# Two-layer hybrid encoder on one core: RWKV blocks moved ahead of the two attention mixers, and an expert loop body of four experts in place of two

## The chip, the cores and the metric

The kernel runs on one core of a Trainium2 chip, in one launch. The metric is the device time of one execution in microseconds (us); the median of several runs is compared. The engines are named as the profile names them: PE is TensorE (matmuls), PEld its weight loads, DVE is VectorE, ACT is ScalarE, POOL is GpSimd and SP is SyncE, which here only issues DMA. "Granted clock" is the share of TensorE's full clock of 2.4 GHz that it was allowed: 1.00 is 2.4 GHz, 0.50 is 1.2 GHz.

## The reference

256 prompt tokens and 32 tokens of a later stream (288 columns in all) pass through two layers of width 1024. Each layer has four token mixers side by side, a gated sum of them, and a feed-forward part.

```python
def prompt_layer(x, p, l):                      # sample_layer: the same with carried states
    h = rmsnorm(x, p['norm_mix'][l])
    za, zb, zc, zd, zg = split_at(h @ p['w_in'][l], TOP_SIZES)
    ya, ... = rwkv_mixer(za, ...)               # A: recurrence over the tokens, then per-head norm
    yb = dsa_prompt(q, qi, wi, k, v, ki, ...)   # B: attention on the keys an indexer selects
    yc, ... = pool_mixer(zc, ...)               # C: causal pooling
    yd, ... = swa_prompt(qd, kd, vd, ...)       # D: sliding-window attention with sinks
    x = x + merge_branches((ya, yb, yc, yd), zg, p, l)
    x = x + channel_mix(x, p, l)

def merge_branches(branches, zg, p, l):
    gates = sigmoid(zg)                         # one gate per branch and channel
    m = sum(gates[i] * (branches[i] @ p['w_branch'][l, i]) for i in range(4))
    return m @ p['w_out'][l]
...
# channel_mix: layer 0 a dense SwiGLU (2816 wide); layer 1 the top 2 of 8 SwiGLU experts (3584 wide)
```

## The kernel before

Everything is written out by hand: each engine has its own program, in order, and semaphores tie them together. The activations are kept transposed, channels on partitions and the 288 tokens along the free dimension, so a layer's `h` is eight tiles of 128x288. The mixers' weights come as sheets of 128x1024; SP loads three sheets (1.5 MB) into one of four ring slots, in the order of the list `SHEETS`, and a slot is loaded again when PE has gone past it. PE uses the sheets in the same order.

Order of PE in a layer before the change. First the input projections (18 tiles, L502 through `in_tiles`) and, by the same helper, the eight gate tiles of branch A (`gates_a`), whose sigmoids are kept in `gate_a`. Then `attn_prep` (L551 on: copies of keys and transposes of values), in layer 0 also `flip_table` (L569, the relative-position table turned round), then `attention` (six steps from the list `STEPS`: three of D, three of B), then three `rwkv_block`s (tokens 0 to 127, 128 to 255, and the 32 of the stream), then the norm of the RWKV output (`head_sums` twice on PE, L537, with `head_norm` on DVE and ACT between and behind them), then A's eight branch products (`branch_part`, L666), then the output projection (`out_tiles`, L502 again).

The latency of attention and RWKV is covered with other branches' work. A fill is a gate tile of a branch (`gate_part`, L647: 8 weight tiles, 16 matmul instructions in the trace since each 32-bit product is two), its sigmoid on ACT (L1244, into the two buffers `sig2`), its branch product (`branch_part`, L666) and its merge on DVE (`merge`, L1679 to L1682: `m += gate * product`; the first branch merged writes `m` with one operation, the others need two). Before the change the D steps are filled with branch C, the B steps with D, the RWKV blocks with B, and A stands at the end with nothing beside it. A fill needs its branch's mixer to be finished, so the order of the mixers and the order of the fills are one choice.

`head_norm` on DVE: L1745 takes the mean off (after the first `head_sums`), L1747 reads the variance (after the second), L1748 to L1752 scale, with a reciprocal of 576 columns (L1750), and signal `y_0_made`. `prep` on DVE is L1576 to L1579, four copies out of PSUM.

In layer 1 the experts run two at a time. `expert(it2, h, first, last)` is one of a pair, written out in full for 14 pairs of column groups (L952 to L983 on PE); PE, ACT and DVE run pair 0, then a loop over pairs, then the last pair:

```python
with pe.Fori(1, final) as it2:        # final is 3 here: two passes, pairs 1 and 2
    expert(it2, 0, False, False)
    expert(it2, 1, False, False)
expert(final, 0, False, False)
```

SP has a loop of its own for the expert weights.

## Time and profile before

| what | us |
|---|---|
| median of three runs (lowest, highest) | 2129.51 (2125.21, 2129.67) |
| the profiled execution: its own time | 2131.87 |
| its span, first to last instruction | 2130.0 |
| PE busy / DVE busy / ACT busy | 2036.5 / 1420.3 / 1019.2 |
| layer 0, end of `gates_a` to the first output tile | 257.95 |
| layer 1, the same stretch | 251.47 |

The span is one chain in which PE does nearly all of the work; the times are positions in it. All stretches below are in us from the span's start. In the two rows on stretches lie `attn_prep`, the attention steps, the RWKV blocks, their norm and A's products: what the change puts in another order.

### The profile page before, as it was taken

The numbers are of one execution on the slowest core, as the hardware profiler recorded it, in microseconds if no ns is written. First come the engines' busy times: TensorE is split into PE (matmuls) and PEld (weight loads), VectorE is DVE, ScalarE is ACT, GpSimd is POOL, SyncE is SP. The second block draws the span as 40 slices with busy tenths as digits, with TensorE's granted clock in tenths as the row PEclk, the third lists the DMA queues.
The fourth block names the chain that finished last, engine by engine and source line by source line (L and its number), as shares of the span: only waits on it lengthen the run. The fifth ranks groups of instructions, "written<-read, shape, count | busy, mean of one in ns | idle before, by whom it ended". The sixth has DMA issues, their size and how long they took to land.

```text
span 2130.0 us, 27280 instructions
## 1 busy us (share of the span) xinstructions
PE 2036.5 (96%) x10340; PEld 1647.0 (77%) x10340; DVE 1420.3 (67%) x1750; ACT 1019.2 (48%) x1170; POOL 140.5 (7%) x108
## 2 busy tenths in 40 slices
PE   7999999889998999998889999999999999999998
PEld 5767687689997777686668787888877888787886
DVE  1445633367873445632378898988887888898987
ACT  1334311043331324311057676767666676676765
POOL 2000000154540000000000000000000000000000
PEclk9999999889999999999979999999999999999999
DMA  7322101324443323201349898899988999898995
GB/s 282 117 76 119 55 36 65 135 95 173 161 164 119 124 96 119 84 26 46 132 156 357 339 352 333 353 340 351 342 332 323 338 349 345 341 357 330 358 348 212
DMA packets 61582, 467.38 MB, mean 219 GB/s; under 512 B 7592, under 2 KB 7848, under 8 KB 9744
## 3 DMA queue, kind: packets, MB, share of 16 engines
q1 hardware_dynamic: 58896, 459.86, 57.2%
q0 software_dynamic: 2560, 5.85, 0.8%
q8 instruction: 78, 1.28, 0.2%
q14 instruction: 48, 0.39, 0.1%
HBM read 462.66 MB, written 3.02 MB: 219 GB/s over the span
## 4 chain that ended last, share of the span: by engine, by line
PE 90%; DVE 5%; ACT 2%; issue 1%; DMA 1%; POOL 0%; SPq 0%; DVEq 0%; ACTq 0%; POOLq 0%
PE ps L502 13%; PE ps L952 10%; PE ps L957 9%; PE ps L954 9%; PE ps L647 8%; PE ps L977 5%; PE ps L978 5%; PE ps L983 5%; PE ps L666 3%; PE ps L843 2%; PE ps L847 2%; PE ps L850 2%; PE ps L921 1%; PE ps L866 1%; PE ps L868 1%
## 5 line engine op out<-in xcount | busy, mean ns | idle before, releaser
L1891 DVE TENSOR_TENSOR ring_r<-ring,unit_hi 128x2048 fp32r<-128x2048 f32 x288 | 653.1, 2290 | 116.3 <-ACT unit_hi L1370 114.0
L1370 ACT ACTIVATE unit_hi<-ring 128x2048 fp32r<-128x2048 f32 x288 | 543.0, 1914 | 4.3 <-issue 3.3
L952 PE MATMUL ps<-unit_hi,hg_hi 128*128 128x512 f32 x896 | 251.1, 402 | 3.0 <-issue 3.0
L954 PE MATMUL ps<-unit_hi,hg_lo 128*128 128x512 f32 x896 | 241.7, 392 | 0.0
L502 PE MATMUL ps<-h,ring 128*128 128x288 f32 x832 | 211.4, 416 | 10.1 <-DVE h L1483 10.1
L647 PE MATMUL ps<-h,ring 128*128 128x288 f32 x768 | 216.5, 421 | 1.7 <-ACT arena L1200 1.0
L957 PE MATMUL ps<-ring_r,hg_hi 128*128 128x512 f32 x772 | 211.8, 396 | 0.0
L502 PEld LDWEIGHTS ps<-h,ring 128*128 128x128 f32 x832 | 162.1, 195 | 57.7 <-issue 11.9
L954 PEld LDWEIGHTS ps<-unit_hi,hg_lo 128*128 128x128 f32 x896 | 168.8, 188 | 37.4
L952 PEld LDWEIGHTS ps<-unit_hi,hg_hi 128*128 128x128 f32 x896 | 160.7, 189 | 38.4 <-issue 8.0
L977 PE MATMUL ps<-unit_hi,h_e_hi 128*128 128x512 f32 x448 | 179.2, 400 | 6.2 <-DVE h_e_lo L1907 6.2
L978 PE MATMUL ps<-unit_hi,h_e_lo 128*128 128x512 f32 x448 | 177.0, 395 | 0.0
L647 PEld LDWEIGHTS ps<-h,ring 128*128 128x128 f32 x768 | 141.5, 194 | 40.8 <-issue 4.0
L957 PEld LDWEIGHTS ps<-ring_r,hg_hi 128*128 128x128 f32 x772 | 145.1, 188 | 33.8 <-DVE ring_r L1891 0.2
L1379 ACT ACTIVATE h_e_hi<-ps 128x256 fp32r<-128x256 f32 x112 | 43.1, 385 | 198.6 <-PE ps L965 198.6
L1891 DVE TENSOR_TENSOR unit_r<-unit,unit_hi 128x2048 fp32r<-128x2048 f32 x48 | 109.9, 2290 | 18.3 <-ACT unit_hi L1370 17.3
L426 POOL TENSOR_TENSOR w_lo<-ring,w_hi 128x1024 fp32r<-128x1024 f32 x44 | 107.8, 2451 | 127.7 <-ACT w_hi L1306 127.6
L977 PEld LDWEIGHTS ps<-unit_hi,h_e_hi 128*128 128x128 f32 x448 | 84.7, 189 | 28.3 <-issue 9.3
L983 PE MATMUL ps<-ring_r,h_e_hi 128*128 128x512 f32 x380 | 104.1, 395 | 0.0
L1782 DVE TENSOR_TENSOR x<-x,ps 128x288 f32<-128x288 f32 x176 | 71.0, 454 | 43.4 <-PE ps L868 43.2
L978 PEld LDWEIGHTS ps<-unit_hi,h_e_lo 128*128 128x128 f32 x448 | 84.9, 190 | 18.0
L1375 ACT ACTIVATE e_gate<-ps 128x256 f32<-128x256 f32 x112 | 43.2, 386 | 104.2 <-PE ps L957 104.2
(385 smaller groups left out, 2826.9 us busy)
## 6 DMA issues: line engine op xcount, KB each, us to landing
ring<-in_w_exp SPq DMA_DIRECT2D x288, 1024.0 KB, 4.9
ring<-in_w_mix SPq DMA_DIRECT2D x44, 1536.0 KB, 6.5
unit<-in_w_exp SPq DMA_DIRECT2D x48, 1024.0 KB, 4.8
ring<-in_w_ffn SPq DMA_DIRECT2D x22, 1536.0 KB, 6.3
rel_table<-rel_row POOLq DMA_DIRECT2D x8, 256.0 KB, 8.9
const<-in_const SPq DMA_DIRECT2D x1, 1186.0 KB, 8.4
x<-in_xT SPq DMA_DIRECT2D x1, 1152.0 KB, 5.2
out_yT<-x SPq DMA_DIRECT2D x4, 288.0 KB, 2.2
```

The lines of the kernel that those rows point to most:

```text
L426: nc.gpsimd.tensor_tensor(w_lo[:, r], slot[:, (MIX + i) % RING, q, :], w_hi[:, r].bitcast(F32), ALU.subtract).then_inc(s["gu_lo_made"], 1)
L502: i = mm(ps[:, bank, 0:T], w[:, k, :], src[:, k], start=(k == 0), stop=(k == KD - 1))
L647: i = mm(ps[:, 0, 0:T], w[:, k, :], h[:, k], start=(k == 0), stop=(k == KD - 1))
L952: mm(out, hg_hi[:, hp, 4 * w + k, :], hi[:, 512 * k:512 * k + 512], start=(w == 0 and k == 0), stop=False)
L954: mm(out, hg_lo[:, hp, 4 * w + k, :], hi[:, 512 * k:512 * k + 512], start=False, stop=False)
L957: z = mm(out, hg_hi[:, hp, 4 * w + k, :], lo[:, 512 * k:512 * k + 512], start=False, stop=(w == 1 and k == 3))
L977: mm(out, eh_hi[:, c], hi[:, cols], start=(j == 0 and c == 0), stop=False)
L978: mm(out, eh_lo[:, c], hi[:, cols], start=False, stop=False)
L983: z = mm(ps[0:CAP, 3 + 2 * h + half, :], eh_hi[:, c], lo[:, cols], start=False, stop=(j == PAIRS - 1 and c == 1))
L1370: fn(unit_hi(q), unit(q), ACT.Copy).then_inc(s["uhi_made"], 1)
L1782: v.tensor_tensor(x[:, d], x[:, d], ps[:, 4 + d % 4, 0:T], ALU.add).then_inc(s["ffn_added"], 1)
L1891: v.tensor_tensor(unit_lo(q), unit(q), unit_hi(q).bitcast(F32), ALU.subtract).then_inc(s["ulo_made"], 1)
```

## The change

A table `ORDER = (2, 0, 3, 1)` now says in which order the branches are merged: C, A, D, B. `LAST` is B. The eight gate tiles made ahead (`gates_a`) are B's; the RWKV blocks come first and are filled with C; D's steps are filled with A, B's steps with D as before, and B's branch products stand at the end. The RWKV norm falls between the blocks and the attention: half of A's first gate tile is put between its two sums on PE, `attn_prep` follows (its transposes split, since the variance sums hold banks 4 and 5), and in the first D step A's first branch product waits until the second gate tile is done. On ACT and DVE the calls are moved alike; on DVE `prep` stands behind all of `head_norm`. The loop over expert pairs takes two pairs in a pass, on PE, ACT and DVE.

```diff
+ORDER = (2, 0, 3, 1)
+LAST = ORDER[3]
+SHEETS = [("in", t) for t in range(18)] + [("gate", LAST, d) for d in range(KD)]
+for _i in ORDER[0:3]:
...
-STEPS = [("D", 0, 2, (0, 1, 2), None), ("D", 1, 2, (3, 4, 5), None), ("D", 2, 2, (6, 7), 0),
+STEPS = [("D", 0, 0, (0, 1, 2), None), ("D", 1, 0, (3, 4, 5), None), ("D", 2, 0, (6, 7), 0),
...
             def attn_prep():
                 pe.wait_ge(s["qk_made"], n("qk_made"))
-                pe.wait_ge(s["y_2_made"], n("y_2_made"))
...
                 for b, (t0, nt) in enumerate(BLK):
-                    for q, src in enumerate((zq[:, 2], zv, zk)):
-                        i = nc.tensor.transpose(ps[0:nt, 4 + q, 128 * b:128 * b + 128], src[:, t0:t0 + nt], ident)
+                    for bank, src in ((6, zq[:, 2]), (7, zv)):
+                        nc.tensor.transpose(ps[0:nt, bank, 128 * b:128 * b + 128], src[:, t0:t0 + nt], ident)
+                pe.wait_ge(s["var_eps"], n("var_eps"))
+                for b, (t0, nt) in enumerate(BLK):
+                    i = nc.tensor.transpose(ps[0:nt, 4, 128 * b:128 * b + 128], zk[:, t0:t0 + nt], ident)
                 i.then_inc(s["prep_full"], 1)
...
             def attention(l):
                 for i, (kind, b, br, tiles, ahead) in enumerate(STEPS):
                     first, last = tiles[0], tiles[-1]
-                    gate_part(l, br, first, 0, 2)
+                    gate_part(l, br, first, 4 if i == 0 else 0, 4 if i == 0 else 2)
...
-                    branch_part(l, br, first)
+                    if i:
+                        branch_part(l, br, first)
                     if len(tiles) == 3:
                         gate_part(l, br, tiles[1], 0, 8)
+                        if i == 0:
+                            branch_part(l, br, first)
                         branch_part(l, br, tiles[1])
...
-                with pe.Fori(1, final) as it2:
+                with pe.Fori(1, pe.snap(final - 1), 2) as it2:
                     expert(it2, 0, False, False)
                     expert(it2, 1, False, False)
+                    then2 = pe.snap(it2 + 1)
+                    expert(then2, 0, False, False)
+                    expert(then2, 1, False, False)
...
                 gates_a(l, 4, 8)
+                pe.wait_ge(s["y_2_made"], n("y_2_made"))
+                for b in range(3):
+                    rwkv_block(l, b)
+                head_sums(oT, 2, None, "mu_full")
+                gate_part(l, 0, 0, 0, 4)
+                head_sums(t1, 4, "oc_sq", "var_full")
                 attn_prep()
                 if l == 0:
                     flip_table()
                 attention(l)
-                for b in range(3):
-                    rwkv_block(l, b)
-                head_sums(oT, 2, None, "mu_full")
-                head_sums(t1, 4, "oc_sq", "var_full")
-                pe.wait_ge(s["y_0_made"], n("y_0_made"))
                 for d in range(KD):
-                    branch_part(l, 0, d)
+                    branch_part(l, LAST, d)
                 out_tiles(l)
```

Where the instructions stand now. First PE, layer 0, behind the last RWKV block in the kernel before: the two sums for the norm, then A's branch products (`y_a` is A's output, `ring` holds weights, `t` is the squares).

```order
L826 MATMUL ps<-arena,state 128x32
L537 MATMUL ps<-y_a,const 128x288 [waits O_up,S_up]
L537 MATMUL ps<-y_a,const 128x288
L537 MATMUL ps<-t,const 128x288 [waits oc_sq]
L537 MATMUL ps<-t,const 128x288
L666 MATMUL ps<-y_a,ring 128x288 [waits merged,y_0_made]
L666 MATMUL ps<-y_a,ring 128x288
L666 MATMUL ps<-y_a,ring 128x288 [waits merged]
```

The same place on PE in the changed kernel (L539 is what L537 was, L651 the gate tiles, L672 the branch products; a row's line numbers are those of the changed file).

```order
L539 MATMUL ps<-y_a,const 128x288 [waits O_up,S_up]
L539 MATMUL ps<-y_a,const 128x288
L651 MATMUL ps<-h,ring 128x288 [waits sig_made,ring_full_0]
L651 MATMUL ps<-h,ring 128x288 x3
L539 MATMUL ps<-t,const 128x288 [waits oc_sq]
L539 MATMUL ps<-t,const 128x288
L556 MATMUL ps<-zq,const 128x288 [waits qk_made]
...
L563 MATMUL ps<-const,zk 128x128 [waits var_eps]
...
L573 MATMUL ps<-rel_table,const 128x512 [waits table_in,prep_made]
```

The wait for `y_0_made` is gone from this place; behind the sums stand the transposes of `attn_prep`, and the first matmul after them waits for `prep_made`. In the first D step of the changed kernel the wait for A's output has come to stand behind the second gate tile:

```order
L651 MATMUL ps<-h,ring 128x288 [waits flip_made]
L600 MATMUL ps<-zq 128x128 x4
L651 MATMUL ps<-h,ring 128x288 x3
L651 MATMUL ps<-h,ring 128x288 [waits sig_made]
L651 MATMUL ps<-h,ring 128x288 x7
L672 MATMUL ps<-y_a,ring 128x288 [waits merged,y_0_made]
L672 MATMUL ps<-y_a,ring 128x288
L672 MATMUL ps<-y_a,ring 128x288 [waits merged]
L672 MATMUL ps<-y_a,ring 128x288
L619 MATMUL ps<-const,arena 128x128 [waits prob_made]
```

L600 are the logits and L619 the transposes of the probabilities; two branch products now stand one right behind the other. On DVE, at the end of the RWKV part of layer 0 in the changed kernel, the four copies that signal `prep_made` (L1592 to L1595, `prep`) follow the whole norm:

```order
L1761 SCALAR_TENSOR_TENSOR y_a<-ps,y_a 128x576 [waits mu_full]
L1763 TENSOR_SCALAR kk<-ps 128x576 [waits var_full]
L1764 TENSOR_TENSOR y_a<-y_a,gate_g 128x576
L1766 RECIPROCAL kk<-kk 128x576 [waits gn_rt,dve_step]
L1767 TENSOR_TENSOR y_a<-y_a,kk 128x576 [waits dve_step]
L1768 TENSOR_TENSOR y_a<-y_a,bonus 128x576 [waits dve_step]
L1592 COPY arena<-ps 128x256 [waits prep_full]
L1593 COPY arena<-ps 32x128
L1594 COPY arena<-ps 128x8
L1595 COPY arena<-ps 32x4
```

Before the change the norm's six operations were followed by the merges of branch A.

## Rows read from the trace of the kernel before

**Rows 1.** The page, part 1: busy time, share of the span, instructions of each engine
```profile
PE 2036.5 (96%) x10340; PEld 1647.0 (77%) x10340; DVE 1420.3 (67%) x1750; ACT 1019.2 (48%) x1170; POOL 140.5 (7%) x108
```

**Rows 2.** Busy time by stretch; PEclk is the granted clock, the last columns DMA
```profile
135.97:393.92 257.95, 235.00 (x1418) 176.99 (x1418) 119.55 (x271) 70.41 (x159) 1.07 (x2) 0.94 0.14 57
147.90:256.80 108.90, 103.10 (x548) 75.68 (x548) 64.98 (x162) 42.70 (x98) 0.00 (x0) 0.97 0.19 73
367.56:381.08 13.52, 4.55 (x9) 2.36 (x9) 7.45 (x6) 2.87 (x4) 0.32 (x1) 0.50 0.06 21
381.08:393.92 12.84, 11.53 (x32) 7.61 (x33) 7.30 (x16) 0.00 (x0) 0.00 (x0) 0.76 0.00 0
777.67:1029.14 251.47, 229.25 (x1403) 175.34 (x1402) 119.52 (x271) 65.62 (x151) 1.07 (x2) 0.93 0.15 58
781.78:892.08 110.30, 104.49 (x549) 76.87 (x549) 64.94 (x162) 42.70 (x98) 0.00 (x0) 0.95 0.19 72
```

**Rows 3.** PE in order of time, layer 0, from the end of the RWKV blocks
```profile
367.96 2.26 PE L537 MATMUL ps<-y_a,const 128*128 128x288 f32 x4 [0.41 <-ACT y_a L1292]
371.78 2.29 PE L537 MATMUL ps<-t,const 128*128 128x288 f32 x4 [1.56 <-ACT t L1297]
381.08 11.72 PE L666 MATMUL ps<-y_a,ring 128*128 128x288 f32 x32 [7.01 <-DVE y_a L1752]
```

**Rows 4.** DVE in order of time: the norm, two of A's merges, and `prep` earlier
```profile
374.11 0.76 DVE L1747 TENSOR_SCALAR kk<-ps 128x576 f32<-128x576 f32 x1 [3.10 <-PE ps L537]
380.26 0.76 DVE L1752 TENSOR_TENSOR y_a<-y_a,bonus 128x576 f32<-128x576 f32 x1
390.55 0.46 DVE L1681 TENSOR_TENSOR gate_a<-gate_a,ps 128x288 f32<-128x288 f32 x1
392.83 0.46 DVE L1681 TENSOR_TENSOR gate_a<-gate_a,ps 128x288 f32<-128x288 f32 x1
...
139.07 0.42 DVE L1576 COPY arena<-ps 128x256 f32<-128x256 f32 x1 [8.95 <-PE ps L559]
139.68 0.14 DVE L1579 COPY arena<-ps 32x4 f32<-32x4 f32 x1
```

**Rows 5.** PE in order of time, layer 0, from `gates_a` to the first D step
```profile
136.47 0.75 PE L555 MATMUL ps<-zq,const 64*128 64x288 f32 x2 [0.50 <-ACT gate_a L1179]
...
140.08 7.13 PE L569 MATMUL ps<-rel_table,const 128*128 128x512 f32 x16 [1.05 <-ACT arena L1200]
147.90 2.69 PE L647 MATMUL ps<-h,ring 128*128 128x288 f32 x10 [0.69 <-ACT rel_table L1456]
```

**Rows 6.** PE in order of time, layer 0: first instructions of the three RWKV blocks
```profile
256.80 1.47 PE L718 MATMUL ps<-ar,bt 64*128 64x256 f32 x8 [0.31 <-ACT kk L1236]
...
300.67 1.13 PE L718 MATMUL ps<-ar,bt 64*128 64x256 f32 x8 [0.56 <-ACT y_a L1292]
...
342.89 0.41 PE L718 MATMUL ps<-ar,bt 64*32 64x64 f32 x8 [0.56 <-ACT y_a L1292]
```

**Rows 7.** PE, the wait in the last B step of layer 0, and stretches with their clock
```profile
247.00 1.14 PE L615 MATMUL ps<-const,arena 32*128 32x32 f32 x12 [3.44 <-DVE arena L1649]
...
247.00:254.40 7.40, 7.40 (x28) 5.12 (x28) 0.17 (x1) 2.23 (x4) 0.00 (x0) 0.54 0.00 1
367.10:387.60 20.50, 11.52 (x25) 7.37 (x26) 9.63 (x11) 2.87 (x4) 0.78 (x2) 0.51 0.04 14
```

**Rows 8.** Busy time by stretch: the expert loop's first pass, and its second with the jump
```profile
1354.84:1610.83 255.99, 255.66 (x1155) 206.24 (x1154) 221.39 (x176) 180.20 (x155) 0.00 (x0) 1.00 0.91 345
1610.83:1873.18 262.35, 257.51 (x1155) 207.35 (x1154) 221.36 (x176) 180.08 (x155) 0.00 (x0) 0.99 0.91 343
```

**Rows 9.** PE and ACT in order of time, at the jump back of the expert loop
```profile
1614.37 1.17 PE L952 MATMUL ps<-unit_hi,hg_hi 128*128 128x512 f32 x4 [2.44 <-issue]
1614.71 1.92 ACT L1370 ACTIVATE unit_hi<-ring 128x2048 fp32r<-128x2048 f32 x1 [3.35 <-issue]
1619.85 1.11 ACT L1392 ACTIVATE y_hi<-ps,w_slot 128x1024 fp32r<-128x1024 f32 x1 [3.23 <-issue]
```

More of the change, by code:

```diff
@@ L88 @@
 NCC = _at
-SHEETS = [("in", t) for t in range(18)] + [("gate", 0, d) for d in range(KD)]
-for _i in (2, 3, 1):
+ORDER = (2, 0, 3, 1)
+LAST = ORDER[3]
+SHEETS = [("in", t) for t in range(18)] + [("gate", LAST, d) for d in range(KD)]
+for _i in ORDER[0:3]:
     for _half in range(2):
         SHEETS += [("branch", _i, _half)] + [("gate", _i, d) for d in range(4 * _half, 4 * _half + 4)]
-SHEETS += [("branch", 0, 0), ("branch", 0, 1)] + [("out", d) for d in range(KD)]
+SHEETS += [("branch", LAST, 0), ("branch", LAST, 1)] + [("out", d) for d in range(KD)]
 SHEET_AT = {k: n for n, k in enumerate(SHEETS)}
 assert len(SHEETS) == 3 * MIX
-STEPS = [("D", 0, 2, (0, 1, 2), None), ("D", 1, 2, (3, 4, 5), None), ("D", 2, 2, (6, 7), 0),
+STEPS = [("D", 0, 0, (0, 1, 2), None), ("D", 1, 0, (3, 4, 5), None), ("D", 2, 0, (6, 7), 0),
          ("B", 0, 3, (0, 1, 2), 1), ("B", 1, 3, (3, 4, 5), 2), ("B", 2, 3, (6, 7), None)]
@@ L635, in gate_part @@
             def gate_part(l, br, d, k0, k1):
[L637 removed]
+                done = KD * ORDER.index(br) + d
                 key = ("gate", br, d)
@@ L654, in branch_part @@
             def branch_part(l, br, d):
-                done = KD * (2, 3, 1, 0).index(br) + d
-                if br == 0:
+                done = KD * ORDER.index(br) + d
+                if br == 0 and d == 0:
+                    pe.wait_ge(s["y_0_made"], n("y_0_made"))
+                if br == LAST:
                     if d % 4 == 0:
@@ L676, in attention @@
                         index_scores(ahead)
-                    gate_part(l, br, first, 2, 5)
+                    gate_part(l, br, first, 4 if i == 0 else 2, 5)
                     if ahead is not None:
@@ L707, in fill @@
                 def fill(q, k0, k1):
-                    gate_part(l, 1, tiles[q], k0, k1)
+                    gate_part(l, 2, tiles[q], k0, k1)
                 t0, nt = BLK[b]
@@ L774, in rwkv_block @@
                 if b < 2:
-                    branch_part(l, 1, tiles[1])
+                    branch_part(l, 2, tiles[1])
                     fill(2, 0, 2)
@@ L789, in rwkv_block @@
                 else:
-                    branch_part(l, 1, tiles[1])
+                    branch_part(l, 2, tiles[1])
                 pe.wait_ge(s["GM_up"], n("GM_up"))
@@ L815, in rwkv_block @@
                 if b < 2:
-                    branch_part(l, 1, tiles[2])
+                    branch_part(l, 2, tiles[2])
                 for j in range(2):
@@ L1285, in rwkv_block @@
                 if b == 2:
-                    sigmoid(l, 1, 3 * b + 1)
+                    sigmoid(l, 2, 3 * b + 1)
                 act.wait_ge(s["QT_full"], n("QT_full"))
@@ L1289, in rwkv_block @@
                 if b < 2:
-                    sigmoid(l, 1, 3 * b + 2)
+                    sigmoid(l, 2, 3 * b + 2)
                 act.wait_ge(s["O_full"], n("O_full"))
@@ L1426, in experts @@
                 final = act.value_load(npass[0:1, 1:2], min_val=3, max_val=11)
-                with act.Fori(1, final) as it2:
+                with act.Fori(1, act.snap(final - 1), 2) as it2:
                     expert(it2, 0, False, False)
                     expert(it2, 1, False, False)
+                    then2 = act.snap(it2 + 1)
+                    expert(then2, 0, False, False)
+                    expert(then2, 1, False, False)
                 expert(final, 0, False, False)
@@ L1451, in _ @@
                 gates_a(2, 8)
+                for b in range(3):
+                    rwkv_block(l, b)
+                head_norm()
                 prep()
@@ L1457, in _ @@
                 attention(l)
-                for b in range(3):
-                    rwkv_block(l, b)
-                head_norm()
                 norm("out_added", KD * l + 1, 1)
@@ L1718, in rwkv_block @@
                     if lv == 3:
-                        merge(l, 1, 3 * b, 3 * b + 1)
+                        merge(l, 2, 3 * b, 3 * b + 1)
                 dve.wait_ge(s["GH_up"], n("GH_up"))
@@ L1726, in rwkv_block @@
                 i.then_inc(s["GM_up"], 1)
-                merge(l, 1, 3 * b + 1, 3 * b + 2)
+                merge(l, 2, 3 * b + 1, 3 * b + 2)
                 dve.wait_ge(s["AT_full"], n("AT_full"))
@@ L1740, in rwkv_block @@
                 if b < 2:
-                    merge(l, 1, 3 * b + 2, 3 * b + 3)
+                    merge(l, 2, 3 * b + 2, 3 * b + 3)
             def head_norm():
@@ L1964, in experts @@
                 final = dve.value_load(npass[0:1, 1:2], min_val=3, max_val=11)
-                with dve.Fori(1, final) as it2:
+                with dve.Fori(1, dve.snap(final - 1), 2) as it2:
                     expert(it2, 0, False, False)
                     expert(it2, 1, False, False)
+                    then2 = dve.snap(it2 + 1)
+                    expert(then2, 0, False, False)
+                    expert(then2, 1, False, False)
                 expert(final, 0, False, False)
@@ L1996, in _ @@
                 pool_out()
-                prep()
-                if l == 0:
-                    dve.wait_ge(s["flip_made"], 8)
-                attention(l)
                 for j in range(2):
@@ L2008, in _ @@
                 head_norm()
-                merge(l, 0, 0, 8)
+                prep()
+                if l == 0:
+                    dve.wait_ge(s["flip_made"], 8)
+                attention(l)
+                merge(l, LAST, 0, 8)
                 add_out()
```

27 lines of the change are left out of this document (13 added, 14 removed).

## The prediction

> **What bounds the kernel now.** I read the page first: PE is busy for 2036.5 us [rows 1], so there is little idle time to win, and what there is must be looked for stage by stage. I then cut the two layers' mixer parts into stretches (busy time by stretch, with the granted clock) and followed PE in order of time inside them. From the end of `gates_a` to the first output tile layer 0 takes 257.95 us and layer 1 251.47 us [rows 2]; there the end of one mixer decides when PE may go on. The worst stretch is 367.56 to 381.08, the RWKV norm: 13.52 us with 4.55 us of matmuls, at a granted clock of 0.50 [rows 2]. PE waits 1.56 us for the squares and then 7.01 us for `y_a`, and then does A's products [rows 3], whose stretch of 12.84 us has a clock of 0.76 [rows 2]. The last place is the expert loop: its second pass is longer than the first by 262.35 - 255.99 = 6.36 us [rows 8]. After the jump back PE stands 2.44 us and ACT 3.35 and 3.23 us on "issue" [rows 9], that is, waiting for nothing that the profile shows. Everything below is positions and differences from these rows; the sum is made against the profiled execution's 2131.87 us (span 2130.0), which lies 2.36 us above the median of the runs, 2129.51.
>
> **The change part by part.** I rebuild the stretch from `gates_a` to the first output tile in its new order.
>
> *Into the RWKV blocks.* PE waits for the last gate's sigmoid as it does now: 0.50 us [rows 5]. `y_2_made` is not a new wait: the pooling output is a DVE result that precedes, in program order, what `prep` did at 139.07 [rows 4], with 8.95 us of DVE idle time in between.
>
> *The blocks.* Block 0 takes 43.87 us now (256.80 to 300.67), block 1, the same work, 42.22 (300.67 to 342.89) [rows 6]. Block 0 follows the last B step, in which PE waited 3.44 us and then ran at a clock of 0.54 for 7.40 us [rows 7]; in the new order it follows a full-speed stretch, so I give it 42.22 too. Block 2 with the wait for its output is 342.89 to 367.96 [rows 6, 3], 25.07. Sum 109.5. The fills' merges are one DVE operation shorter here and one longer in the D steps; DVE is busy for 64.98 of 108.90 us there [rows 2], so I count both at nothing; if the D steps' eight extra operations of 0.46 us [rows 4] were all exposed, they would cost 3.7 a layer.
>
> *The norm and `attn_prep`.* This is where the stall goes. PE: mean sums, half a gate tile, variance sums, transposes; then it waits for `prep_made`. On DVE `prep` is queued behind the whole norm, and behind `prep` on PE stands all of the attention (in layer 0 the table turn). From the variance sums' end to the norm's end is 374.11 to 381.02, 6.91 us; `prep` itself 139.07 to 139.82, 0.75 [rows 4]; 0.08 for the signal: 7.74 us that PE can't shorten, of which it fills some 3 us with the transposes (now 136.47 to 139.03, before the wait of 1.05) [rows 5]. Ahead of that stand the sums, 2.26 and 2.29 us at half clock [rows 3], about half of it at full clock, and eight gate instructions, 2.1 us (2.69 for ten [rows 5]), or 4.2 at half clock. At full clock all the way: 1.1 + 2.1 + 1.1 + 7.7 = 12.0. At half clock: 2.3 + 4.2 + 2.3 + 7.7 = 16.5. The clock is already low when the sums start now, and rose again after some 7 us of steady matmuls both times [rows 7], so I take a middle of 14.6. The squares' wait of 1.56 us [rows 3] is hidden by the gate instructions; without them it would be there again.
>
> *The table turn, layer 0 alone*: 140.08 to 147.90, 7.82, as before [rows 5].
>
> *A slow start of the attention.* PE stands for 14.6 less 10 or so, 4 to 5 us, before `prep_made`. A wait of 3.44 us was followed by 7.40 us at 0.54 [rows 7], which is some 3.4 us of lost time; the wait in the norm now is followed by half clock until 387.6 [rows 7]. No row shows a shorter loss after a wait of that length, but part of the slow time may lie in the wait itself. Bounds: 0 (the clock stays) and 10.2 (20.50 us at half clock [rows 7], all of it under matmuls). I take 2.5, near the shorter case, since matmuls run up to 5 us before the attention and not 7.
>
> *The attention steps.* 108.90 and 110.30 us now [rows 2]. Half a gate tile is gone from the first step: -2.1. In that step the branch product no longer covers the sigmoid between two gate tiles: +0.5, as ahead of the transposes now [rows 5]. The two branch products then stand back to back and share one bank, so the second waits for the first one's merge, two operations of 0.46 with their signals, 1.2; and DVE does that merge before the probabilities, about 0.2 more. Together -0.2: 108.7 and 110.1. `y_0_made` comes before `prep` on DVE and delays nothing.
>
> *The end.* B's products replace A's, with no norm ahead of them. Their pace is that of the merges: two in 2.28 us (390.55 to 392.83) [rows 4], so eight take 9.1, and the first product's four instructions 1.0 [rows 5]: 10.1. At half clock they take what A's take, 12.84 [rows 2]. The last B step has its wait and slow clock as before, so some of that falls here: I take 11.4.
>
> *Sum.* Layer 0: 0.5 + 109.5 + 14.6 + 7.8 + 2.5 + 108.7 + 11.4 = 255.0 against 257.95, a gain of 2.9. Layer 1: 0.5 + 109.5 + 14.6 + 2.5 + 110.1 + 11.4 = 248.6 against 251.47, a gain of 2.9. So about 5.8 in the mixers: of a norm stretch of 13.52 us almost all comes back, since the wait for `y_a` has become a wait for `prep_made` behind the same six DVE operations.
>
> *The expert loop.* With two pairs in a pass and `final` at 3 there is one pass and no jump back: -6.36. Lower bound of the gain 0 (the stalls belong to reading instructions and come elsewhere), upper bound 6.7 (the whole difference of the two passes and the 0.33 us that PE is idle in the first). Entering and leaving the loop shows nothing to pay: the first pass has 255.66 of 255.99 us busy [rows 8]. I take 6.4. The Trainium skill, Advanced Engine Details and Errata, section Control Flow Timing, puts a compare-and-branch at about 108 ns; by that figure the jump would be worth 0.1 us and the whole change 6 us instead of 12, which is the time of the third rival below. The trace disagrees with it here, with 6.36 us. The skill's Runtime: NRT & Kernel Launch, section Instruction fetch mechanics, has the reason that would fit: code is fetched ahead in sequence, and a taken branch whose target isn't held waits for the fetch; no view here shows the fetch itself.
>
> Total: 5.8 + 6.4 = 12.2. 2131.87 - 12.2 = 2119.7, and less the 2.36 by which the profiled execution lies above the median, **2117.3 us**.
>
> **The rivals.**
>
> *The clock stays up.* If the sums, the start of the attention and the end run at 2.4 GHz, each layer gains 2.6 (14.6 to 12.0), 2.5 and 1.3 more: 12.8 in all, 2104.5. For it: the blocks themselves run close to full clock, and the sums are now surrounded by gate matmuls. Against it: the clock is down at the sums already [rows 3], after block 2's small matmuls, which haven't changed.
>
> *The mixers give nothing.* With 16.5 for the norm, 3.4 for the slow start and 12.4 at the end the layers lose 3.8 each of the 2.9: -1.8 together, and with the loop 2125. For it: the chain on DVE is the same as before the change, only the wait has another name.
>
> *The stalls of the jump remain.* If a body twice as long has to wait for its instructions at another place, 6.4 is lost: 2123.7. Against it: in the 255.99 us of the first pass PE is idle for 0.33 us, over the same number of instructions in a row.
>
> *Slower.* The slow clock after `prep_made` lasts as long as the one after the wait for `y_a`: 20.50 us at half clock [rows 7], here with matmuls under all of it, 10.2 us a layer in place of 2.5, and the norm at 16.5: 19 us more, 2136. It decides from about 17 us lost beyond the forecast, some 8 a layer, or 21 us of half clock a layer. Against it: the 20.50 us hold 7.01 us of waiting; the other case ended after 7.40.
>
> **How the numbers follow.** The forecast has 0.50, and for itself 2112 to 2122; the clock staying up 0.19 (in one layer alone it gives 2111); the mixers giving nothing 0.15; the stalls of the jump remaining 0.09; slower 0.05; 0.02 is left for what I don't see. A measurement of this kernel can tell some 0.2% (4.3 us) from no change, so faster means below 2125.2. Faster: the forecast, the clock, two thirds of the stalls' case and half of the mixers' case, 0.83; same 0.11; slower 0.06. The range from 2106 to 2126 leaves out most of the slower case and the half of the clock's case in which both layers gain all of it.
>
> **What would show it.** In the profile after: a PE wait for a DVE copy of `prep` of 4 to 6 us after the variance sums, in both layers; no wait at the branch products before the output projection; 42 to 43 us for each of the first two RWKV blocks; the stretch from `gates_a` to the first output tile near 255 and 249 us; and two passes of the expert loop in 2 x 256 us with no "issue" wait of 2 us on PE or ACT. The prediction is wrong if the granted clock in the first D step stays at 0.5 for more than 10 us, if the clock at the sums is 1.00, or if an "issue" wait shows up inside the longer loop body.

## The result and the profile after

The changed kernel takes 2114.89 us (median of four runs, 2112.24 to 2115.37) against 2129.44 of the kernel before on the same chip (four runs, 2125.21 to 2129.67): a ratio of 0.9926, 95% interval 0.9915 to 0.9938. It is faster by 14.5 us, 2.4 more than forecast. Its profiled execution took 2115.37 us, span 2113.5. The page, part 1, columns as in [rows 1]: PE is busy for 5 us less.

```profile
PE 2031.6 (96%) x10340; PEld 1643.8 (78%) x10340; DVE 1420.0 (67%) x1750; ACT 1023.4 (48%) x1174; POOL 140.6 (7%) x108
```

Busy time by stretch, columns as in [rows 2] (start and end, length, then busy time and instructions of PE, PEld, DVE, ACT and POOL, the granted clock, DMA share and GB/s): the two layers from the end of `gates_a` to the first output tile, layer 0's start of attention and B's products at its end, and the two passes' worth of expert pairs, which is now one pass (from the last step of one pair to that of the next, as in [rows 8]).

```profile
134.66:388.51 253.85, 233.92 (x1418) 175.32 (x1418) 118.07 (x267) 71.63 (x160) 1.07 (x2) 0.96 0.15 58
771.80:1020.02 248.22, 229.19 (x1402) 174.91 (x1402) 118.05 (x267) 66.87 (x152) 1.07 (x2) 0.94 0.15 59
257.58:267.40 9.82, 9.14 (x16) 3.76 (x16) 0.00 (x0) 4.81 (x9) 0.00 (x0) 0.79 0.00 0
378.28:388.51 10.23, 8.81 (x32) 5.60 (x33) 7.30 (x16) 0.00 (x0) 0.00 (x0) 1.00 0.00 0
1345.52:1601.09 255.57, 255.57 (x1155) 206.43 (x1154) 221.10 (x176) 180.08 (x155) 0.00 (x0) 1.00 0.91 345
1601.09:1856.66 255.57, 255.57 (x1156) 206.43 (x1155) 221.10 (x176) 180.03 (x155) 0.00 (x0) 1.00 0.93 351
```

Against [rows 2] layer 0 gains 257.95 - 253.85 = 4.10 us and layer 1 251.47 - 248.22 = 3.25. In the experts PE is busy without a gap. From layer 1's first output tile to the end are 1093.48 us, where the kernel before took 2130.0 - 1029.14 = 1100.86: 7.38 gained. Two stretches that the change does not touch give the rest: up to the end of `gates_a` 134.66 in place of 135.97, and between the two mixer parts 383.29 in place of 383.75. Together 4.10 + 3.25 + 7.38 + 1.31 + 0.46 = 16.5, the difference of the two spans.

PE in order of time, layer 0, from the end of the RWKV blocks (L539 is the norm's sums, L651 gate tiles, L573 the table turn, L672 branch products; in brackets how long the engine was idle ahead of a row, and what ended that):

```profile
244.10 1.80 PE L539 MATMUL ps<-y_a,const 128*128 128x288 f32 x4 [0.40 <-ACT y_a L1305]
245.70 3.24 PE L651 MATMUL ps<-h,ring 128*128 128x288 f32 x8
248.78 1.13 PE L539 MATMUL ps<-t,const 128*128 128x288 f32 x4
...
257.58 9.14 PE L573 MATMUL ps<-rel_table,const 128*128 128x512 f32 x16 [5.18 <-DVE arena L1595]
267.40 0.75 PE L651 MATMUL ps<-h,ring 128*128 128x288 f32 x2 [0.69 <-ACT rel_table L1475]
...
270.95 4.15 PE L651 MATMUL ps<-h,ring 128*128 128x288 f32 x16 [0.50 <-ACT log_decay L1257]
274.94 1.13 PE L672 MATMUL ps<-y_a,ring 128*128 128x288 f32 x4
277.11 1.24 PE L672 MATMUL ps<-y_a,ring 128*128 128x288 f32 x4 [1.04 <-DVE m L1698]
```

The wait of 7.01 us for `y_a` [rows 3] is gone, and one of 5.18 us has come, for the last copy of `prep`. What stands ahead of that copy is seen on DVE, in order of time:

```profile
249.95 0.76 DVE L1763 TENSOR_SCALAR kk<-ps 128x576 f32<-128x576 f32 x1 [3.25 <-PE ps L539]
250.63 0.75 DVE L1764 TENSOR_TENSOR y_a<-y_a,gate_g 128x576 f32<-128x576 f32 x1
251.53 3.75 DVE L1766 RECIPROCAL kk<-kk 128x576 f32<-128x576 f32 x1 [0.15 <-ACT kk L1312]
...
256.78 0.42 DVE L1592 COPY arena<-ps 128x256 f32<-128x256 f32 x1
...
257.39 0.14 DVE L1595 COPY arena<-ps 32x4 f32<-32x4 f32 x1
```

PE's last transpose ended at about 252.4; the copies read nothing of the norm, and yet start at 256.78, behind the reciprocal.

### The profile page after: what moved, and what is told of

Its sections match the earlier page's. It is cut to its first block, busy times and chain, and to the rows that moved or that the text cites. A ratio compares the mean times of both kernels' runs of the same rounds, so it can differ in the third digit from the quotient of the medians.

```text
span 2113.5 us, 27278 instructions
## 1 busy us (share of the span) xinstructions
PE 2031.6 (96%) x10340; PEld 1643.8 (78%) x10340; DVE 1420.0 (67%) x1750; ACT 1023.4 (48%) x1174; POOL 140.6 (7%) x108
## 4 chain that ended last, share of the span: by engine, by line
PE 92%; DVE 5%; ACT 2%; issue 1%; POOL 0%; DMA 0%; DVEq 0%; ACTq 0%; POOLq 0%
PE ps L504 13%; PE ps L961 10%; PE ps L966 10%; PE ps L963 10%; PE ps L651 8%; PE ps L986 5%; PE ps L992 5%; PE ps L987 5%; PE ps L672 3%; PE ps L852 2%; PE ps L856 2%; PE ps L859 2%; PE ps L930 1%; PE ps L974 1%; PE ps L875 1%; PE ps L876 1%
## 5 line engine op out<-in xcount | busy, mean ns | idle before, releaser
L651 PE MATMUL ps<-h,ring 128*128 128x288 f32 x768 | 222.1, 429 | 6.9 <-DVE arena L1595 5.2
L651 PEld LDWEIGHTS ps<-h,ring 128*128 128x128 f32 x768 | 144.6, 199 | 48.2 <-DVE arena L1595 5.5
```

What stands on the lines that cost most here:

```text
L651: i = mm(ps[:, 0, 0:T], w[:, k, :], h[:, k], start=(k == 0), stop=(k == KD - 1))
```

## The experiments

Ten kernels, in three batches, each batch on one chip with its own runs of the kernel before (medians 2130.47, 2128.74 and 2130.74 us; the changed kernel's was 2129.44). Across batches the ratios to before are compared; the stretches come from the profiled executions.

**The two parts apart.** First the kernel before with nothing but the longer loop body (PE is shown; ACT and DVE are changed alike).

```diff
-                with pe.Fori(1, final) as it2:
+                with pe.Fori(1, pe.snap(final - 1), 2) as it2:
                     expert(it2, 0, False, False)
                     expert(it2, 1, False, False)
+                    then2 = pe.snap(it2 + 1)
+                    expert(then2, 0, False, False)
+                    expert(then2, 1, False, False)
```

> The kernel before with the longer expert loop alone; the mixers keep their order. Theory: the jump back cost what the second pass was longer than the first, 6.36 us, and with one pass nothing takes its place: 2122 to 2123.5 us beside 2129.4, a ratio of 0.997; the two pairs of the pass take 256 us each and neither PE nor ACT has an issue wait over 1 us inside it. Rival: the stalls belong to reading code and come at another place of the longer body: no difference, 2129, with issue waits of 2 to 3 us somewhere in the loop.

Measured: 2122.83 us (2118.29 to 2124.66), ratio 0.9960 (0.9947 to 0.9972). The two pairs take 255.56 and 255.57 us, and PE has no gap in them. The stalls of the jump do not come back elsewhere.

Then the new order alone: the changed kernel with the short loop body.

> The changed kernel with the expert loop as before, two experts in a pass; the mixers in the new order. Theory: the order gives the 4.10 and 3.25 us by which the two layers' stretches from the gates to the first output tile became shorter, so 2121 to 2123 us beside 2129.4, and the second loop pass is again 6 to 7 us longer than the first. Rival: part of the gain lies outside these stretches (the start of the profile after is 1.3 us earlier too): 2118 to 2120. With the loop alone the two parts should add up to the whole, 14.5 us.

Measured: 2118.60 us (2117.94 to 2119.20), ratio 0.9946 (0.9933 to 0.9959). The mixer stretches are those of the changed kernel, 253.79 and 248.22 us. The theory's 2121 to 2123 us is missed; the time is the rival's. Of the 12.8 us between the two spans (2130.0 and 2117.2) 1.5 lie ahead of and between the mixers, as the rival says, but 3.9 lie in the expert part (1100.86 to 1096.98), which neither expected. And 7.6 and 11.9 us add up to 19.5, where both together gave 14.5 (each of the three is known to some 2.5 to 3 us). In the profiled executions 3.7 us of the overlap lie at the jump. Busy time by stretch of this kernel, its two passes of the expert loop:

```profile
1345.66:1601.22 255.56, 255.56 (x1155) 206.25 (x1154) 221.06 (x176) 180.19 (x155) 0.00 (x0) 1.00 0.91 346
1601.22:1860.38 259.16, 255.92 (x1155) 206.16 (x1154) 220.99 (x176) 180.10 (x155) 0.00 (x0) 1.00 0.92 347
```

The second is longer by 3.60 us, not by the 6.36 of [rows 8]. PE and DVE in order of time, at the jump:

```profile
1604.52 1.17 PE L961 MATMUL ps<-unit_hi,hg_hi 128*128 128x512 f32 x4 [2.20 <-ACT unit_hi L1380]
...
1607.60 2.29 DVE L1901 TENSOR_TENSOR ring_r<-ring,unit_hi 128x2048 fp32r<-128x2048 f32 x1 [3.51 <-issue]
```

PE and DVE stand; ACT, which stood twice in [rows 9] waiting for nothing, waits here only for PE. The work in the loop is the same. So the price of a jump back is not a constant of the loop.

**Moving code without changing work.** To see whether an engine's place in its code sets that price, 22 one-element copies were put on ACT after layer 0's dense part, in the kernel before. They lie far ahead of the loop and have nothing to do with it.

```diff
                 dense() if l == 0 else experts()
+                for q in range(22 if l == 0 else 0):
+                    fn(small[0:1, 42 + q:43 + q], const[0:1, 0:1], ACT.Copy)
```

> The kernel before, with 22 one-element copies on ACT after layer 0's dense part, where it has nothing to do: all later code of ACT, the expert loop's among it, lies 22 instructions further on. The jump back cost 7.2 us in the kernel before, with ACT standing, and 3.5 with the new order alone, with DVE and PE standing. If the price depends on where an engine's code lies: ACT's two stalls of 3.3 us come elsewhere or not at all, and the time moves by 3 to 7 us (2123 to 2126, or above 2131). If not: 2129, and the stalls stay where they are.

Measured: 2126.77 us (2121.90 to 2128.49, 11 runs) beside 2130.74, ratio 0.9987 (0.9978 to 0.9997), and the two passes are:

```profile
1353.11:1608.67 255.56, 255.56 (x1155) 206.24 (x1154) 221.05 (x176) 180.23 (x155) 0.00 (x0) 1.00 0.91 345
1608.67:1868.02 259.35, 255.97 (x1155) 206.14 (x1154) 220.98 (x176) 180.12 (x155) 0.00 (x0) 1.00 0.92 347
```

ACT, PE and DVE in order of time at the jump:

```profile
1607.29 3.71 ACT L1370 ACTIVATE unit_hi<-ring 128x2048 fp32r<-128x2048 f32 x2
1610.90 1.11 ACT L1392 ACTIVATE y_hi<-ps,w_slot 128x1024 fp32r<-128x1024 f32 x1
...
1612.09 1.19 PE L952 MATMUL ps<-unit_hi,hg_hi 128*128 128x512 f32 x4 [2.32 <-issue]
...
1615.23 2.29 DVE L1893 TENSOR_TENSOR ring_r<-ring,unit_hi 128x2048 fp32r<-128x2048 f32 x1 [3.69 <-issue]
```

ACT's stalls of 3.35 and 3.23 us are gone, PE's 2.32 and one of DVE remain, and the second pass is 3.79 us longer than the first. In the kernel before DVE stood as long at this place, under ACT's name:

```profile
1617.22 2.29 DVE L1891 TENSOR_TENSOR ring_r<-ring,unit_hi 128x2048 fp32r<-128x2048 f32 x1 [3.54 <-ACT unit_hi L1370]
```

So ACT's first stall ran beside one of DVE and its end can have won little; the price fell by 6.36 - 3.79 = 2.57 us, less than ACT's second stall alone. In the median the gain is 4.0 us, by the ratio 2.8 with 0.6 to 4.7 as its interval, at or under the low end of the 3 to 7 expected. Of the 5.2 us between the two spans (2130.0 and 2124.8) 3.5 lie behind layer 1's first output tile, which is what the first theory says; the other 1.7 lie where both kernels run the same instructions. Moving ACT's code took ACT's stalls away, as far as one profiled execution of each layout shows. The new order puts ACT's calls in another order too, which would explain why it takes nearly half of the jump's price with it. The loop's part is worth 7.23 us in the old order (the 1093.63 us from layer 1's first output tile to the end, against 1100.86) and 3.5 in the new (1020.22 to 2117.2, against 1020.02 to 2113.5).

The Trainium skill, Advanced Engine Details and Errata, section Control Flow Timing, has one figure for a compare-and-branch, about 108 ns. The three traces with a jump show 6.36, 3.60 and 3.79 us.

**The new wait.** `prep` moved on DVE ahead of the reciprocal and of the wait for ACT's root:

```diff
-            def head_norm():
+            def head_norm(between):
...
                 then(v.tensor_tensor(oT, oT, gate_g, ALU.mult))
+                between()
...
-                head_norm()
-                prep()
+                head_norm(prep)
```

> The changed kernel with the four prep copies on DVE put ahead of the reciprocal and the two products behind it, right after the variance is read. Theory: PE's wait of 5.18 us for the last of these copies in each layer is DVE's order and not the work: the wait falls to about 1 us, the attention starts some 4.3 us earlier, and since PE stands no longer it keeps the clock of 2.4 GHz and gains 2 us more: 6 us a layer, 2102 to 2104 us against 2114.9 for the changed kernel. Rival: the norm's end is needed by the first D step anyway (its first branch product waits for y_0_made, and the scores stand behind it on DVE), so the wait only moves there in layer 1, where no table turn covers it: 2107 to 2110.

Measured: 2100.62 us (2098.24 to 2101.01), ratio 0.9863 (0.9848 to 0.9877). PE's wait in order of time, and the start of the attention by stretch:

```profile
253.56 7.13 PE L573 MATMUL ps<-rel_table,const 128*128 128x512 f32 x16 [1.05 <-ACT arena L1213]
```

```profile
253.56:270.09 16.53, 15.30 (x52) 8.55 (x52) 7.82 (x10) 11.19 (x22) 0.00 (x0) 1.00 0.16 66
```

The wait is 1.05 us, for ACT's own copies, and the clock stays at 1.00. On DVE the copies now wait 1.14 us for PE's last transpose, and the reciprocal starts 2 us later (253.54 in place of 251.53), for which PE waits nowhere in this kernel; the table turn takes 7.13 where it took 9.14. Of the 17.2 us between the two spans 2 x 4.13 are the wait itself and 2.0 + 1.85 the slow clock right behind it. The other 5 us were in neither theory. Part of them is clock further on: layer 1's input projection, which nothing was done to, takes 112.74 us in the changed kernel and 110.09 here (652.55 to 762.64).

**Is it the wait or the clock behind it?** The changed kernel with its wait left as it is, but PE kept busy with ten matmuls that nobody reads:

```diff
-                pe.wait_ge(s["prep_made"], n("prep_made", 2))
+                pe.wait_ge(s["merged"], 32 * (n("prep_made", 2) // 2 - 1) + 8)
+                for _ in range(10):
+                    mm(ps[:, 1, 0:T], ident, h[:, 0], start=True, stop=True)
+                pe.wait_ge(s["prep_made"], n("prep_made", 0))
```

> The changed kernel, with ten matmuls whose result nobody uses put where PE waits 5.18 us for prep_made, in both layers (5.4 us of work at full clock). What costs there, the wait or the half clock behind it? My theory: the wait is fixed by DVE's chain and stays as long as before under another name, and the half clock that follows it (255.2 to 262.0 and 893.4 to 900.3) is a consequence of PE standing: with PE busy it goes, and each layer gains 2 us behind the wait, the whole about 2111. Rival: the half clock comes from what ran before the wait (the sums), and stays: same time, 2115, or 1 more where the unused matmuls end late.

Measured: 2107.25 us (2104.92 to 2109.67), ratio 0.9896 (0.9881 to 0.9911). Layer 1's first D step shows the direct effect. The changed kernel:

```profile
895.95 1.33 PE L651 MATMUL ps<-h,ring 128*128 128x288 f32 x2 [5.18 <-DVE arena L1595]
...
901.35 4.15 PE L651 MATMUL ps<-h,ring 128*128 128x288 f32 x16 [0.50 <-ACT log_decay L1257]
```

and this one:

```profile
894.18 0.75 PE L654 MATMUL ps<-h,ring 128*128 128x288 f32 x2 [0.33 <-DVE arena L1598]
...
897.73 4.15 PE L654 MATMUL ps<-h,ring 128*128 128x288 f32 x16 [0.50 <-ACT log_decay L1260]
```

From the norm's sums to the first of these rows both kernels take 13.86 us, so the wait is as long as it was under another name. But the eight gate and eight logit instructions from there to the next wait take 3.55 us in place of 5.40. That is the clock alone, and it fell because PE stood: the 2 us a layer expected. The whole gained some 6.5 by the ratios; part of the rest is clock later in layer 1, which this run does not tie to the wait (53.83 us in place of 55.53 from the third D step's wait to the third B step's, 18.27 in place of 21.29 from there to the first output tile).

**The two short waits in the first D step.** A's first branch product back ahead of the second gate tile, in the changed kernel:

```diff
-                    if i:
-                        branch_part(l, br, first)
+                    branch_part(l, br, first)
                     if len(tiles) == 3:
                         gate_part(l, br, tiles[1], 0, 8)
-                        if i == 0:
-                            branch_part(l, br, first)
```

> The changed kernel with the first branch product of the first D step back in its usual place, ahead of the second gate tile. Theory: the move costs a wait of 0.50 us for the sigmoid and one of 1.04 us for the merge in each layer, and since y_0_made is 10 us earlier than the product nothing has to wait for it: 1.5 us a layer, 2111.5 to 2112.5 us against 2114.9. Rival: the product in its usual place makes DVE's merge come ahead of the scores' end and delays the probabilities: no difference, 2114 to 2115.5.

Measured: 2104.49 us (2101.99 to 2105.62), ratio 0.9882 (0.9868 to 0.9896). Both waits, 0.50 and 1.04, are gone in both layers. That is 3.1 us of a gain of some 10, and both expectations are missed. Between the two profiled executions the spans differ by 13.8. Where much of the rest lies is seen in stretches that hold the same instructions in both kernels: layer 1's input projection, and from the third D step's wait to the third B step's. The changed kernel, then this one:

```profile
943.20:998.73 55.53, 52.09 (x277) 37.78 (x277) 46.19 (x120) 22.14 (x48) 0.00 (x0) 0.97 0.29 114
...
659.06:771.80 112.74, 112.63 (x452) 86.43 (x452) 46.42 (x65) 28.83 (x48) 5.33 (x9) 0.98 0.33 118
```

```profile
934.15:987.99 53.84, 50.40 (x276) 36.68 (x277) 46.19 (x120) 22.13 (x48) 0.00 (x0) 1.00 0.30 118
655.98:766.08 110.10, 109.98 (x452) 84.58 (x452) 46.42 (x65) 28.82 (x48) 5.32 (x9) 1.00 0.34 121
```

No instruction differs in these stretches, only their position in time: 1.69 and 2.64 us by the clock alone. The largest piece is the next stretch of layer 1, from the third B step's wait to the first output tile: 21.29 us in the changed kernel (998.73 to 1020.02) and 18.30 here (987.99 to 1006.29). The runs of the two kernels do not overlap, so the gain belongs to the kernel; why the clock fares better in it is not shown.

**A shift and nothing else.** To test that, four unused matmuls were put ahead of RWKV block 0 in layer 0 of the changed kernel.

```diff
                 pe.wait_ge(s["y_2_made"], n("y_2_made"))
+                for _ in range(4 if l == 0 else 0):
+                    mm(ps[:, 1, 0:T], ident, h[:, 0], start=True, stop=True)
```

> The changed kernel with four matmuls whose result nobody uses ahead of RWKV block 0 in layer 0 alone: 2.15 us of work at full clock, all of it on the path, nothing else changed. If the half-clock stretches follow the waits alone, each comes again 2.15 us later and the time is 2115 + 2.2 = 2117. My theory after the last two runs is that the same wait may or may not be followed by half clock, and for 3.4 or 6.8 us, depending on where it falls in time: then some of the stretches behind the 2.05 and 3.44 us waits change, and the time is off 2117 by 2 us or more to either side.

Measured: 2116.06 us (2113.80 to 2118.05), ratio 0.9936 (0.9923 to 0.9950). The total is what the rival expects, about 2 us above the changed kernel. Its stretches are not:

```profile
135.18:393.48 258.30, 238.59 (x1426) 178.72 (x1426) 118.03 (x267) 71.62 (x160) 1.07 (x2) 0.95 0.15 57
...
775.35:1020.77 245.42, 226.27 (x1403) 172.80 (x1402) 118.03 (x267) 66.86 (x152) 1.07 (x2) 0.96 0.16 60
```

Layer 0 is longer by 4.45 us, where 2.15 were added, and layer 1, in which nothing was added, shorter by 2.80. That the total came to the rival's number is two changes of opposite sign. Whether the shift made them is not shown, since executions of the same instructions differ as well. The kernel before, the one with the longer loop alone and the one with ACT's code moved run the same program up to the end of layer 0's mixers. `gates_a` ended in them at 135.97, 133.62 and 133.53 us, and layer 0 took 257.95 [rows 2], 259.47 and 259.20; the last two:

```profile
133.62:393.09 259.47, 236.47 (x1419) 178.33 (x1418) 119.51 (x271) 70.35 (x159) 1.07 (x2) 0.93 0.14 56
...
133.53:392.73 259.20, 236.20 (x1419) 178.25 (x1418) 119.54 (x271) 70.40 (x159) 1.07 (x2) 0.93 0.15 56
```

(The kernel with the new order alone repeats the changed kernel's two stretches within 0.1 us; so two executions can also agree.) With one profiled execution of each kernel, some on different chips, what the shift did and what differs from execution to execution cannot be told apart here.

**The half gate tile between the sums.** Taken out again, so that the tile stands whole in the first D step:

```diff
...
                 head_sums(oT, 2, None, "mu_full")
-                gate_part(l, 0, 0, 0, 4)
                 head_sums(t1, 4, "oc_sq", "var_full")
```

> The changed kernel without the half gate tile between the two sums of the norm (the tile stands whole in the first D step again). By the prediction's terms: the 3.2 us of the half tile there go, the wait of 1.56 us for the squares is back, so the variance sums and with them all of DVE's chain are 1.7 us earlier, and the first D step is 2.1 us longer: 0.4 us a layer, 2116, which can't be told from 2115. Rival: without matmuls there the clock falls lower or for longer, and each layer loses 2 to 3 us more: 2120.

Measured: 2117.54 us (2113.13 to 2120.81), ratio 0.9943 (0.9929 to 0.9956), which can't be told from the changed kernel. The stretches are 0.23 and 0.39 us longer, as expected in sum but not by its terms. The wait for the squares is back:

```profile
247.65 2.29 PE L539 MATMUL ps<-t,const 128*128 128x288 f32 x4 [1.57 <-ACT t L1309]
...
257.60 9.08 PE L573 MATMUL ps<-rel_table,const 128*128 128x512 f32 x16 [3.04 <-DVE arena L1594]
```

The variance sums start 1.13 us earlier, but at half clock, and end at the same time; PE resumes at 257.60 in place of 257.58. So the half tile costs the norm nothing, since the sums and transposes behind it run at full clock. The first D step is 1.92 us shorter with it; all but 0.28 of that comes back here further on in the layer, in stretches that are the same in both.

**Both mends together**, `prep` first and the branch product back:

> Both mends together: prep ahead of the reciprocal on DVE, and A's first branch product back ahead of the second gate tile. If both work as waits alone: 2100.6 from the first, less 0.50 and 1.04 in layer 0; in layer 1 y_0_made is now late, since prep and the reciprocal stand ahead of it, so the first product waits some 2 us in place of 1.54: about 2099.5. Rival, by which the second mend's 10 us were mostly half-clock stretches that went away wherever the steps fell: again 5 to 8 us, 2092 to 2096, or nothing.

Measured: 2098.29 us (2097.44 to 2103.86), ratio 0.9855 (0.9841 to 0.9868): between the two expectations, and not to be told from the first mend alone (0.9863). The new wait in layer 1 is there as worked out:

```profile
895.90 1.24 PE L672 MATMUL ps<-y_a,ring 128*128 128x288 f32 x4 [2.32 <-DVE y_a L1766]
```

The profiled execution was the slowest of the five, 2103.86, and shows why: in layer 0 the stretch from RWKV block 2's first instruction to its wait of 0.52 us (219.12 to 245.79) took 26.67 us at a clock of 0.74, where the changed kernel's took 20.51 (219.62 to 240.13). Nothing was edited ahead of this stretch: one execution of the same instructions lost 6 us to the clock.

**Keeping PE busy in two older waits.** The 2.05 and 3.44 us in the third D and B steps are in the kernel before as well. On top of both mends:

```diff
                 t0, nt = BLK[b]
+                for _ in range({"D": 4, "B": 6}[kind] if b == 2 else 0):
+                    mm(ps[:, 7, 0:T], ident, h[:, 0], start=True, stop=True)
                 pe.wait_ge(s["prob_made"], n("prob_made"))
```

> Both mends, and in the third D step and the third B step of either layer unused matmuls where PE waits 2.05 and 3.44 us for the probabilities (four and six of them, 2.2 and 3.2 us at full clock, so that PE goes on when it did). My theory: the half clock behind these two waits comes from PE standing; with PE busy it stays up there, which gives back 2 to 3 us a layer: 2093 to 2095 against 2098. Rival: the half clock comes from the short matmuls around the wait, and stays: 2098.

Measured: 2091.72 us (2089.29 to 2094.76), ratio 0.9828 (0.9812 to 0.9843), the fastest of all. The stretch from the wait in the third B step to the first output tile, layer 0, with both mends alone and then with PE kept busy:

```profile
365.96:387.35 21.39, 19.80 (x81) 13.53 (x81) 8.21 (x18) 2.45 (x5) 0.00 (x0) 0.76 0.00 1
```

```profile
358.93:375.68 16.75, 15.01 (x80) 10.44 (x81) 8.21 (x18) 2.45 (x5) 0.00 (x0) 1.00 0.00 1
```

4.64 us for the same work (21.50 with the first mend alone). In layer 1 little clock was left to win (18.29 to 18.02). The theory's 3 to 5 us became 6 by the ratios.

## Why the prediction was right, and where its sizes were off

The terms, in us, as forecast and as the changed kernel's PE rows give them:

| term | forecast | layer 0 | layer 1 |
|---|---|---|---|
| wait ahead of the blocks | 0.5 | 0.50 | 0.50 |
| RWKV blocks | 109.5 | 108.94 | 109.79 |
| norm and `attn_prep` until PE resumes | 14.6 | 13.48 | 13.86 |
| table turn and slow start (layer 0) | 7.8 + 2.5 | 9.82 | |
| attention steps (with slow start in layer 1) | 108.7 / 112.6 | 110.88 | 112.57 |
| B's products | 11.4 | 10.23 | 11.50 |
| sum | 255.0 / 248.6 | 253.85 | 248.22 |

*The wait moves and does not go.* Right in all points: 5.18 us for a copy of `prep`, in both layers, no wait over 0.31 us at the branch products ahead of the output projection, and the norm no shorter: from the first of the sums until PE goes on behind its long wait 13.12 us before (367.96 to 381.08 [rows 3]) and 13.48 now, with half a gate tile and the transposes in it. What the prediction did not say is that the wait was not forced by the data. `prep` stands behind the norm in DVE's program alone, and moving four copies gave another 14 us, about as much as the whole change.

*The clock at the sums.* One sign of being wrong came in part: the variance sums ran at full clock in both layers, 1.13 us where they had taken 2.29 [rows 3]; the mean's took 1.80 in layer 0 and 2.26 in layer 1. Without the half gate tile between them the variance sums took 2.29 again, so it is the half tile that brings the clock up. The prediction took a middle of 12.0 and 16.5, and 13.48 and 13.86 lie below it.

*The slow start* was forecast at 2.5 between bounds of 0 and 10.2, and was 9.82 - 7.82 = 2.00 in layer 0 and 5.40 - 3.55 = 1.85 in layer 1. That PE's standing causes it is shown by the run with PE kept busy.

*The attention steps.* The 0.50 for the sigmoid was exact, and of the 1.2 for the merge 1.04 was seen. Layer 0's steps took 2.2 us more than forecast. The clock was 0.53 from 312.81 to 320.00, behind the 2.05 us wait, where the kernel before kept 1.00 behind the same wait (rows of both below); that is some 3.4 us, and half as much was won back behind the 3.44 us wait (0.73, before 0.54 [rows 7]). But the 108.90 us that this term was built on were one execution's: the same instructions took 110.38 us with the longer loop alone (145.55 to 255.93) and 110.14 with ACT's code moved (145.46 to 255.60). So some 1.2 to 1.5 of the 2.2 can lie in the number that was started from. That layer 0 as a whole came within 1.2 us is luck in part: the steps were too low by 2.2, the blocks, the norm and the end too high by 0.6, 1.1 and 1.2. Layer 1 came out to 0.03 us.

*The end.* In layer 0 B's products ran at 1.00 and took 10.23, near the lower bound of 10.1; in layer 1 at 0.85 and took 11.50. The clock staying up was a rival for whole layers; it held at this place in one layer.

*The loop* was mis-sized: forecast 6.4 with 6.7 as its upper bound, and 7.4 gained from the first output tile of layer 1 to the end (7.23 with the loop alone). The second pass shrank by 6.78, and the first by 0.42 although nothing jumps into it; the upper bound had counted 0.33 for that. The rest, 0.2, lies outside the two passes. The term holds for both parts of the change together; behind the new order alone the longer body is worth 3.5.

*Outside the terms* are 1.31 us at the start and 0.46 between the layers, which the sum held at nothing. The first is clock: the 32 matmul instructions of the input projection at 66.06 took 9.72 us in the kernel before, and the same 32, at 66.44, 8.03 in the changed one. It is not the change's: they took 8.03 as well with the longer loop alone and with ACT's code moved, where nothing ahead of them differs from the kernel before.

Between the two profiled executions the gain is 16.5 where 12.2 was forecast: 1.5 more in the mixers, 1.0 in the loop and 1.8 outside. The medians give 2 of it back, since the profiled execution before lay 2.4 above its median and the one after 0.5.

## What to carry to other kernels

When a step is moved in one engine's program, look on every other engine at what it now stands behind: PE waited 5.18 us for four copies that needed nothing of the reciprocal ahead of them. A wait on PE costs its length and, often, the slow clock behind it, and where no useful work fits, matmuls that nobody reads can save the second part (some 6 us here for ten matmuls a layer). And a gain of a few microseconds in such a kernel should be read stage by stage: stretches that the edit did not touch moved by 1 to 3 us each, executions of the same instructions differed by as much and once by 6, so one profile of each kernel does not say which it was. The price of the loop's jump fell from 6.36 to 3.79 us when code elsewhere moved.

## What had not been expected of the hardware

*One wait, several prices.* The granted clock (the column ahead of the last two) in the 6 to 7 us right behind the 2.05 us wait, of the same instructions; before, layer 0 and 1:

```profile
193.17:200.00 6.83, 6.83 (x44) 5.05 (x48) 6.21 (x27) 2.34 (x5) 0.00 (x0) 1.00 0.00 0
...
827.05:834.00 6.95, 6.95 (x36) 5.13 (x36) 6.33 (x27) 2.12 (x4) 0.00 (x0) 0.75 0.01 4
```

Layer 0 again, the same program up to there, with the longer loop alone and with ACT's code moved:

```profile
190.82:197.65 6.83, 6.83 (x34) 4.99 (x34) 6.21 (x27) 2.12 (x4) 0.00 (x0) 0.75 0.00 0
...
190.73:197.56 6.83, 6.83 (x35) 5.07 (x35) 6.21 (x27) 2.12 (x4) 0.00 (x0) 0.75 0.00 0
```

The changed kernel, layer 0 behind the 2.05 us wait, then behind the 3.44 us wait, and layer 1 likewise:

```profile
312.81:320.00 7.19, 7.19 (x24) 4.87 (x24) 6.16 (x27) 2.12 (x4) 0.00 (x0) 0.53 0.00 1
370.07:376.50 6.43, 6.43 (x34) 4.73 (x34) 0.76 (x2) 2.22 (x4) 0.00 (x0) 0.73 0.00 0
...
943.20:949.50 6.30, 6.30 (x30) 4.52 (x30) 5.72 (x26) 2.12 (x4) 0.00 (x0) 0.73 0.00 0
998.73:1006.00 7.27, 7.27 (x27) 5.02 (x27) 0.05 (x1) 2.22 (x4) 0.00 (x0) 0.53 0.00 0
```

It runs from 0.53 to 1.00 behind the same wait, in layer 0 of one and the same program from 0.75 to 1.00. In time that is up to some 3 us each. The Trainium skill, TensorE: Matmul & The Clock Gate, Part 1, says that the block that sets the clock looks at PE's activity in a window that runs freely, not tied to the kernel; that would fit, and no view here shows the window. What stays open is what sets the price in a given execution: no run here was made to forecast one.

*A jump back has several prices*: 6.36, 3.60 or 3.79 us for the same loop, in one profiled execution each, with ACT stalling for 3.35 and 3.23 us in one layout and not at all in two others. That the engine waits for its instructions there is argued from these rows and not shown; no view has the fetch itself.
